# First products of a conformer/MoE block on x laid out turned and unscaled, later turned rows mostly through ScalarE, and strip groups from the highest down

## The chip, the cores and the metric

One core of a Trainium2 chip runs the whole program. The metric is the device time of one execution, in microseconds (us). A gain or a loss is told against the median of the runs of the kernel before.

## What is computed

One residual block on x of 1024 tokens by 1024 channels, float32. The lines of the reference that matter here:

```python
u = rms_norm(h, norm1_g)
proj = u @ w_in                                   # 1024 x 1792
conv_out = conformer_conv_group(proj[..., :c0], ...)   # GLU, 31 taps, LayerNorm, swish
attn_out = swa_sink_attention(q, k, v, ...)       # 8 heads, windows of two chunks
h = h + concatenate([conv_out, attn_out]) @ w_out
v = rms_norm(h, norm2_g)
h = h + moe(v, ...)                               # top 4 of 32 experts, clamped SwiGLU
```

The RMS norm divides each token's row by its root mean square and multiplies each channel by norm1_g. The division is one number per token, the gain one per channel. A product `u @ w_in` is therefore the product of `x * norm1_g` with the weights, each token's row of the result then scaled by its own number.

## The kernel before, in words

P is 128. Tokens are cut into 8 tiles of 128 (t), channels into 8 tiles of 128 (k), and tokens also into two halves of 512 (h). The program is written by hand: each of the five engines has its own list of instructions, run in order, and semaphores tie them together. SyncE (SP) issues the loads, in program order, on one queue.

**Start.** SP loads x tiles 0 to 3 into `xin`, then 128 gate and 128 value columns of w_in (`load_cv(0, 0, P)`), nine small rows, x tiles 4 to 7, b1, router weights, sinks and router bias (`small`), then the other columns of w_in. ScalarE squares each x tile with a sum (L599), GpSimd turns the sum into a reciprocal root (L450, L451), VectorE scales the tile (`norm_x`, L927). TensorE turns it in 128x128 blocks (`trans_first` L1306, `trans_u` L1332) into PSUM banks. ScalarE and VectorE take half of the banks each into `uT`, with the gain (`take_uT`, L604 and L932). `gated` (L1342) multiplies 128 columns of w_in with a half of uT: the gate side and the value side of a unit. A unit is one channel tile c of the convolution and one half h, numbered i = 2c + h, so there are eight. Units 0 and 1 are made at the start (EARLY = 2), six more in the attention loop. `turn_cols` (L1313, L1315) and `turn_b1` (L1322) turn small vectors into columns.

**Convolution.** A unit's gate goes through a sigmoid on ScalarE (`take_gate`, L620), the value is copied (`take_val`, L623), and GpSimd multiplies the two into `zT` (`glu`, L489). ScalarE writes tap 0 (`tap_zero`, L628). The other 30 taps are multiply-adds on VectorE (`tap`, L982), one after another, over 512 tokens or over both halves at once (1024). `some_taps(n, ...)` issues taps until 2n halves are done; the calls are placed by hand between other duties of VectorE.

**Attention.** A loop over s, the eight token tiles. TensorE's order in a step: `proj_kv(s+1)` (L1388), gate product of a unit, `trans_q(s)` (L1398, L1401), `proj_q(s+1)` (L1378), value product, `scores(s)` (L1416), with the turns of probabilities and the product with v of the step before. `trans_q(s)` waits for `qn_ready`, which VectorE gives in `norm_qk(s)`: a sum (L995), 2.5 (that is 3 double) taps while GpSimd takes the root (L450, L451), and two multiplications (L1002, L1005). Step 0 has VectorE issue `some_taps(16)`, `norm_qk(0)`, three more groups of taps and `norm_qk(1)`.

**Experts.** After the routing a table of passes is made on VectorE (L1169 to L1196), its end is one product on TensorE. Then a loop over passes: each takes up to 256 tokens of one expert, in widths n of 96 to 256. Hidden products (L1243) fill the time, then `down_rows` for the first 128 tokens (L1260, two halves of the columns) and `down_quads` for the others (L1278), in strips of 32 tokens; a strip group g is one such strip, in bank 3 or 7 by `quad_bank(g)`. ScalarE takes each result with its gate (L570, L577), VectorE adds the bias (L903, L910), and GpSimd adds rows to the output in DRAM by indirect DMAs: `add_rows` (L430), and, in passes that are not 128 wide, four `add_quads` (L434), one for each group, used or not. In before the groups go from 0 up: the unused ones are the last.

```python
            if n >= P:
                down_rows(0)
                down_rows(1)
...
                down_quads(range((SLOTS - n) // QG_ROWS - QUADS, QUADS) if n < P else range(-(-(n - P) // QG_ROWS)))
```

## Time and profile before

| | |
|---|---|
| median of 3 runs | 1938.51 us (1937.95 to 1939.67) |
| the profiled execution's own time | 1937.04 us |
| its span in the trace | 1935.3 us, so 1.7 us lie around it |
| granted TensorE clock, mean | 0.994 |
| TensorE (PE) busy | 98% of the span |
| VectorE (DVE) busy | 53% |
| ScalarE (ACT) busy | 23% |
| GpSimd (POOL) busy | 25% |
| moved by DMA | 519 MB, 268 GB/s over the span |

All times are us from the start of the span. A row of the chain of waits is a piece of the work that ended last, followed back. A timeline row begins with the start and the length of a run of equal instructions; in brackets stands the idle time before it and what ended it. A row of windows gives, for a stretch, the busy time of PE, of its weight loads (PEld), DVE, ACT and POOL, then the granted clock (1.00 is 2.4 GHz, 0.50 is 1.2 GHz), the DMA engines' share and GB/s.

### The profile page before, as it was taken

How to read it: one execution, taken by the hardware profiler on the slowest of the kernel's cores; microseconds unless marked ns; L12 is line 12 of the kernel's file. 1: busy time of each engine (PE TensorE's matmuls, PEld its weight loads, DVE VectorE, ACT ScalarE, POOL GpSimd, SP SyncE). 2: the span in 40 equal slices, each digit the busy share in tenths (PEclk: the TensorE clock that was granted, in tenths of full speed). 3: DMA queues.
4: the chain of work that ended last, by engine and by line, in shares of the span. 5: the costliest groups of instructions: out<-in, count | busy, mean ns of one | idle time of the engine just before them, and what ended most of it. 6: DMA issues, size and time to landing. Idle time of an engine off the chain costs nothing.

```text
span 1935.3 us, 35973 instructions
## 1 busy us (share of the span) xinstructions
PE 1900.7 (98%) x12864; PEld 1447.9 (75%) x12865; DVE 1027.2 (53%) x2836; ACT 440.0 (23%) x966; POOL 479.3 (25%) x446
## 2 busy tenths in 40 slices
PE   8999999989999999999999999999999999999997
PEld 5555554458888877888887777888888888778995
DVE  5999973365555545555554444444444444335542
ACT  4357582121111111211111111111111111111110
POOL 3110100011122211211222133333333332323333
PEclk9999999989999999999999999999999999999999
DMA  7000226348999999999999999999999998879992
GB/s 249 1 1 1 66 65 236 113 175 292 343 348 354 341 354 353 352 345 338 355 354 341 345 318 325 313 310 310 310 309 304 314 296 283 261 239 359 348 355 48
DMA packets 250502, 518.92 MB, mean 268 GB/s; under 512 B 13457, under 2 KB 30893, under 8 KB 250448
## 3 DMA queue, kind: packets, MB, share of 16 engines
q1 hardware_dynamic: 223392, 453.50, 65.0%
q0 software_dynamic: 27040, 64.66, 13.5%
q8 instruction: 39, 0.64, 0.1%
q14 instruction: 15, 0.12, 0.0%
q10 hardware_dynamic: 16, 0.00, 0.0%
HBM read 483.49 MB, written 34.62 MB: 268 GB/s over the span
## 4 chain that ended last, share of the span: by engine, by line
PE 93%; DVE 4%; ACT 1%; DMA 1%; POOL 1%; issue 1%; DVEq 0%; POOLq 0%
PE bank L1243 51%; PE bank L1260 21%; PE bank L1466 6%; PE bank L1342 4%; PE bank L1278 4%; DVE arena L982 2%; PE bank L1378 2%; PE bank L1388 1%; DMA arena<-token_rows,idx_q 1%; PE bank L1416 1%; PE bank L1636 1%; PE bank L1491 0%; PE bank L1569 0%; PE bank L1440 0%; PE bank L1306 0%
## 5 line engine op out<-in xcount | busy, mean ns | idle before, releaser
L1243 PE MATMUL bank<-arena 128*128 128x128 f32 (+6 forms) x8192 | 1001.3, 284 | 2.6 <-ACT arena L803 1.3
L1243 PEld LDWEIGHTS bank<-arena 128*128 128x128 f32 x8192 | 986.6, 191 | 16.8 <-issue 13.1
L425 POOL DMA_INDIRECT arena<-token_rows,idx_q x256 | 250.0, 977 | 638.5 <-PE bank L1243 592.6
L1260 PE MATMUL bank<-arena 128*128 128x512 f32 x928 | 403.0, 592 | 0.0
L1260 PEld LDWEIGHTS bank<-arena 128*128 128x128 f32 x928 | 174.3, 190 | 208.1 <-issue 208.1
L841 DVE TENSOR_SCALAR arena<-bank,b1c 128x256 f32<-128x256 f32 x256 | 123.8, 484 | 374.4 <-PE bank L1243 370.0
L562 ACT ACTIVATE arena<-arena 128x256 f32<-128x256 f32 x256 | 106.7, 417 | 832.5 <-DVE arena L841 832.5
L982 DVE SCALAR_TENSOR_TENSOR arena<-arena,cols 128x512 f32<-128x512 f32 (+1 forms) x226 | 182.3, 807 | 12.8 <-ACT arena L628 5.8
L890 DVE STREAM_TRANSPOSE arena<-arena 128x256 f32<-128x256 f32 x256 | 87.3, 408 | 190.5 <-DMA arena<-token_rows,idx_q 190.5
L430 POOL DMA_INDIRECT out<-arena,idx_cur x32 | 56.0, 1750 | 412.7 <-DVE arena L903 366.5
L853 DVE SCALAR_TENSOR_TENSOR arena<-arena 128x256 f32<-128x256 f32 x256 | 108.9, 425 | 38.0 <-DVE arena L850 9.8
L570 ACT ACTIVATE arena<-bank,gate_cur 128x512 f32<-128x512 f32 x64 | 43.6, 686 | 351.2 <-PE bank L1260 351.2
L843 DVE TENSOR_SCALAR arena<-bank,b1c 128x256 f32<-128x256 f32 x256 | 121.6, 475 | 0.0
L434 POOL DMA_INDIRECT out<-arena,idxq_cur x68 | 108.9, 1602 | 41.0 <-DVE arena L910 25.4
L1466 PE MATMUL bank<-arena 128*128 128x512 f32 x256 | 115.6, 599 | 0.8 <-ACT arena L699 0.8
L1342 PE MATMUL bank<-arena 128*128 128x512 f32 x256 | 113.2, 595 | 0.3 <-DVE arena L932 0.3
L850 DVE TENSOR_TENSOR arena<-arena 128x256 f32<-128x256 f32 x256 | 107.4, 419 | 2.9
L1278 PE MATMUL bank<-arena 128*32 128x256 f32 x1664 | 93.3, 380 | 0.0
L903 DVE SCALAR_TENSOR_TENSOR arena<-arena,gate_cur 128x512 f32<-128x512 f32 x64 | 47.9, 752 | 80.8 <-ACT arena L570 69.6
L1342 PEld LDWEIGHTS bank<-arena 128*128 128x128 f32 x256 | 47.5, 190 | 55.0 <-issue 54.6
L1466 PEld LDWEIGHTS bank<-arena 128*128 128x128 f32 x256 | 46.8, 190 | 52.7 <-issue 52.6
L1278 PEld LDWEIGHTS bank<-arena 128*32 128x32 f32 x1664 | 52.3, 110 | 43.7 <-issue 10.6
(240 smaller groups left out, 1089.5 us busy)
## 6 DMA issues: line engine op xcount, KB each, us to landing
arena<-in_w SPq DMA_DIRECT2D x192, 2048.0 KB, 13.5
arena<-in_b SPq DMA_DIRECT2D x32, 512.0 KB
arena<-in_x SPq DMA_DIRECT2D x16, 512.0 KB, 5.8
token_rows<-arena SPq DMA_DIRECT2D x8, 576.0 KB, 3.2
out<-arena SPq DMA_DIRECT2D x8, 512.0 KB, 6.0
arena<-in_b SPq DMA_DIRECT2D x128, 32.0 KB
arena<-token_rows,idx_q POOLq DMA_INDIRECT x256
arena<-in_w_in SPq DMA_DIRECT2D x2, 1536.0 KB, 10.7
```

The source lines that it names most:

```text
L425: pool.indirect_dma_start(out=gath_q[:, g, :], out_offset=None, in_=quads_d, in_offset=bass.IndirectOffsetOnAxis(ap=idx_q[:, g:g + 1], axis=0)
L434: pool.indirect_dma_start(out=out_q, out_offset=bass.IndirectOffsetOnAxis(ap=idxq_cur[:, g:g + 1], axis=0), in_=ytq[:, g, :], in_offset=No ...
L841: v.tensor_scalar(g1[:, r, :], bank[r][:, 0:SLOTS], b1c[:, m:m + 1], LIMIT, ALU.add, ALU.min).then_inc(g1_ready, 1)
L843: v.tensor_scalar(l1[:, r, :], bank[r][:, SLOTS:], b1c[:, MT + m:MT + m + 1], LIMIT + 1.0, ALU.add, ALU.min).then_inc(hid_free, 1)
L850: v.tensor_tensor(tt[:, r, :], g1[:, r, :], sg[:, r, :], ALU.mult).then_inc(dve_loop, 1)
L853: v.scalar_tensor_tensor(act[:, m, :], l1[:, r, :], 1.0 - LIMIT, tt[:, r, :], ALU.max, ALU.mult).then_inc(act_ready, 1)
L982: link(v.scalar_tensor_tensor(out_, zT[:, c, lo + j:lo + j + n], col(CW + c * WIDTH + j), out_, ALU.mult, ALU.add))
L1243: last = mm(bank[m % 2][:, side * SLOTS + at:side * SLOTS + at + n], w1_sb[:, k, lo:lo + P], xT[:, k, at:at + n], start=k == 0, stop=k == ...
L1260: last = mm(bank[4 + b][:], act[:, m, 0:P], w2_sb[:, m, b * HALF:(b + 1) * HALF], start=m == 0, stop=m == MT - 1)
L1278: last = mm(dst[j * QG_ROWS:(j + 1) * QG_ROWS, at:at + D // 4], act[:, m, lo:lo + QG_ROWS], w2_sb[:, m, j * (D // 4):(j + 1) * (D // 4)], ...
L1342: last = mm(dst[:], w_cv[:, k, lo:lo + P], uT[:, k, h * HALF:(h + 1) * HALF], start=k == 0, stop=k == KD - 1)
L1466: last = mm(bank[mixed_bank(t) + b][:], src, w_o[:, k, b * HALF:(b + 1) * HALF], start=part_ == 0 and i == 0, stop=part_ == 1 and i == CT - 1)
```

## The change

Four things change together.

**First products.** The host lays out x turned (`x_turned`, channels by tokens) and the first 2x128 columns of w_in, tile by tile (`w_first`). SP loads half 0 of the turned x straight into `uT`, in eight pieces, then the value side of w_first; ScalarE's queue loads the gate side. VectorE multiplies each piece by the gain in place (`apply_gain`). The products of units 0 and 1 so run on unnormed x. The token's factor comes later: `spread_x` (four transposes of a broadcast column for each half) puts the factors of all tokens on all partitions, ScalarE copies them to `rsB`, and GpSimd multiplies gate and value by them before the sigmoid and the GLU (`early_glu`, three multiplications a half instead of one). The x tiles themselves are loaded too, tiles 0 to 3 before half 1 of the turned x and tiles 4 to 7 behind it.

**Later turned rows.** `uT` is then written again from turned, normed tiles, half 0 (`trans_u(0)`) after both early units, half 1 (`trans_u(1)`) in step 0 of the attention loop, behind `trans_q(0)`. Of each four turned groups ScalarE takes three and VectorE the fourth: its `take_uT(3)` and `take_uT(7)` stand behind 12 taps, `take_uT(11)` and `take_uT(15)` behind `norm_qk(0)`. ScalarE norms x tiles 4 to 7, VectorE tiles 0 to 3. `proj_kv(0)` waits for all groups of half 0.

**Constants.** norm, bias, tap and b1 vectors come laid out as columns: `turn_cols`, `turn_b1` and their nine loads go. b1 and router weights are loads of 128 long rows. q/k/v columns of w_in are loaded before the rest of the gate and value columns.

**Experts.** Strip groups go from 3 down: groups 3 and 2 between the two row halves, 1 and 0 behind them, on all engines; unused groups are now the first. In the table, two reductions (`dead`, `wraps`) move behind `diag_ready`.

```diff
+            for k in range(KD):
+                sp.dma_start(uT[:, k, 0:HALF], x_turned[k * P:(k + 1) * P, 0:HALF]).then_inc(xt0_in[k], 16)
+            for b in range(2):
+                load_first(sp, 0, b)
             load_x(range(4))
-            load_cv(0, 0, P)
-            for dst, src in as_rows:
-                sp.dma_start(dst, src).then_inc(rows_in, 16)
+            for b in range(KD // 2):
+                sp.dma_start(uT[:, 2 * b:2 * b + 2, HALF:], x_turned[2 * b * P:2 * (b + 1) * P, HALF:]
+                             .rearrange("(k p) s -> p k s", p=P)).then_inc(xt1_in[b], 16)
             load_x(range(4, NT))
             for dst, src in small:
                 sp.dma_start(dst, src).then_inc(small_in, 16)
-            load_cv(1, P, D_CONV - P)
             sp.dma_start(w_qkv, w_in[:, 2 * D_CONV:].rearrange("(k p) n -> p k n", p=P)).then_inc(wqkv_in, 16)
+            for side in (1, 0):
+                at = side * D_CONV + P
+                sp.dma_start(w_cv[:, :, at:at + D_CONV - P], ...).then_inc(wcv_in, 16)
...
+            def apply_gain(k, h):
+                u = uT[:, k, h * HALF:(h + 1) * HALF]
+                v.tensor_scalar(u, u, col(G1 + k), None, ALU.mult).then_inc(gained, 1)
...
+            def early_glu(h):
+                half = slice(h * HALF, (h + 1) * HALF)
+                pool.wait_ge(rs_spread, h + 1)
+                pool.wait_ge(glu_ev, 2 * (h + 1))
+                pool.tensor_tensor(sigb[:, h, :], sigb[:, h, :], rsB[:, half], ALU.mult).then_inc(gate_scaled, 1)
+                link(pool.tensor_tensor(valb[:, h, :], valb[:, h, :], rsB[:, half], ALU.mult))
+                pool.wait_ge(early_sig, h + 1)
+                pool.tensor_tensor(zT[:, 0, PAD + h * HALF:PAD + (h + 1) * HALF], sigb[:, h, :], valb[:, h, :], ALU.mult
+                                   ).then_inc(z_ready, 1)
...
-            some_taps(16, EARLY)
+            some_taps(6, EARLY)
+            for g in range(3, KD, 4):
+                take_uT(g)
+            some_taps(8, EARLY)
             norm_qk(0, EARLY)
+            for g in range(KD + 3, 2 * KD, 4):
+                take_uT(g)
...
+            def all_turned(h):
+                pe.wait_ge(ut_act, 6 * (h + 1))
+                pe.wait_ge(ut_dve, 2 * (h + 1))
+            def trans_u(h):
+                pe.wait_ge(u_ready, 4 * (h + 1))
...
+                for g in range(h * KD, (h + 1) * KD):
+                    if g >= 4:
+                        if g % 4 < 3:
+                            pe.wait_ge(ut_act, 3 * (g // 4 - 1) + g % 4 + 1)
+                        else:
+                            pe.wait_ge(ut_dve, g // 4)
...
+            gated(0, 1, bank[1])
+            gated(0, 0, bank[0]).then_inc(glu_mm, 1)
+            spread_x(0)
+            gated(1, 1, bank[3])
             gated(1, 0, bank[2]).then_inc(glu_mm, 1)
-            pe.wait_ge(wcv_in[1], 32)
+            trans_u(0)
+            spread_x(1)
...
-                    for g in range(QUADS):
-                        pool.wait_ge(yq_ready, q_quads + g + 1)
+                    for g in reversed(range(QUADS)):
+                        pool.wait_ge(yq_ready, q_quads + QUADS - g)
...
+            if used < QUADS:
+                pe.sem_inc(yq_mm, QUADS - used)
...
+            if used > 2:
+                down_quads((3, 2))
+            if n >= P:
+                down_rows(1)
+            if used > 0:
+                down_quads((1, 0))
```

**TensorE, from its first real work to the attention loop's step 0.** L1306 and L1332 turn x, L1313 to L1322 turn small vectors, L1342 is `gated`, L1388 and L1378 are the first key/value and query products. Before:

```order
L1306 MATMUL bank<-ident,arena 128x128 x32
L1342 MATMUL bank<-arena 128x512 x8
L1313 MATMUL bank<-ident,arena 128x30
L1315 MATMUL bank<-ident,arena 128x31 x4
L1342 MATMUL bank<-arena 128x512 x4
L1332 MATMUL bank<-ident,arena 128x128 x16
L1342 MATMUL bank<-arena 128x512 x4
L1332 MATMUL bank<-ident,arena 128x128 x16
L1322 MATMUL bank<-ident,arena 128x128 x4
L1342 MATMUL bank<-arena 128x512 x16
L1388 MATMUL bank<-arena 128x256 x8
L1378 MATMUL bank<-arena 128x512 x8
```

Now (L1352 is `gated`, L1382 `spread_x`, L1373 `trans_u`, L1422 and L1411 the key/value and query products, L1434 and L1437 `trans_q(0)`):

```order
L1352 MATMUL bank<-arena 128x512 x16
L1382 MATMUL bank<-ident,rs 128x128 x4
L1352 MATMUL bank<-arena 128x512 x16
L1373 MATMUL bank<-ident,arena 128x128 x32
L1382 MATMUL bank<-ident,rs 128x128 x4
L1422 MATMUL bank<-arena 128x256 x8
L1411 MATMUL bank<-arena 128x512 x8
L1422 MATMUL bank<-arena 128x256 x8
L1352 MATMUL bank<-arena 128x512 x8
L1434 MATMUL bank<-ident,arena 128x128 x4
L1437 MATMUL bank<-ident,arena 128x128
L1373 MATMUL bank<-ident,arena 128x128 x32
```

The products of the early units moved ahead of all turns of x; the first 32 turns stand behind them, the other 32 behind `trans_q(0)`.

**VectorE, from the last scaling of a constant to `norm_qk(1)`.** Before (L968 is the last work on b1, L982 are taps, L995, L1002 and L1005 are `norm_qk`):

```order
L968 TENSOR_SCALAR b1T<-b1T 128x32x8
L982 SCALAR_TENSOR_TENSOR arena<-arena,cols 128x512 x16
L982 SCALAR_TENSOR_TENSOR arena<-arena,cols 128x1024 x8
L995 TENSOR_REDUCE ss<-arena 128x10
L982 SCALAR_TENSOR_TENSOR arena<-arena,cols 128x1024 x3
L1002 TENSOR_TENSOR arena<-arena,rs 128x512
L1005 TENSOR_TENSOR arena<-arena,rs 128x128
L982 SCALAR_TENSOR_TENSOR arena<-arena,cols 128x1024 x3
L982 SCALAR_TENSOR_TENSOR arena<-arena,cols 128x512 x16
L995 TENSOR_REDUCE ss<-arena 128x10
```

Now (L1003 the last work on b1, L1017 taps, L987 `take_uT`, L1030, L1037 and L1040 `norm_qk`):

```order
L1003 TENSOR_SCALAR b1T<-b1T 128x32x8
L1017 SCALAR_TENSOR_TENSOR arena<-arena,cols 128x512 x12
L987 TENSOR_SCALAR arena<-bank,cols 128x512 x2
L1017 SCALAR_TENSOR_TENSOR arena<-arena,cols 128x512 x4
L1017 SCALAR_TENSOR_TENSOR arena<-arena,cols 128x1024 x6
L1030 TENSOR_REDUCE ss<-arena 128x10
L1017 SCALAR_TENSOR_TENSOR arena<-arena,cols 128x1024 x3
L1037 TENSOR_TENSOR arena<-arena,rs 128x512
L1040 TENSOR_TENSOR arena<-arena,rs 128x128
L987 TENSOR_SCALAR arena<-bank,cols 128x512 x2
L1017 SCALAR_TENSOR_TENSOR arena<-arena,cols 128x1024 x5
L1017 SCALAR_TENSOR_TENSOR arena<-arena,cols 128x512 x13
```

The four evictions of turned groups moved in between the taps; three of the 46 taps of the first channel tile now run inside `norm_qk(1)`, where none ran before.

## Rows read from the trace of the kernel before

**Rows 1.** The page: busy shares, and the chain by engine.

```profile
PE 1900.7 (98%) x12864; PEld 1447.9 (75%) x12865; DVE 1027.2 (53%) x2836; ACT 440.0 (23%) x966; POOL 479.3 (25%) x446
...
PE 93%; DVE 4%; ACT 1%; DMA 1%; POOL 1%; issue 1%; DVEq 0%; POOLq 0%
```

**Rows 2.** The chain of waits in order of time, 0 to 105 us: start, length, what.

```profile
0.83 3.58 DMA arena<-in_x
...
14.07 7.10 PE bank L1342 x16
...
37.08 0.76 DVE arena L982
...
88.96 0.66 PE bank L1398 x4
```

**Rows 3.** Timeline of TensorE, 45 to 125 us.

```profile
46.17 3.62 PE L1388 MATMUL bank<-arena 128*128 128x256 f32 x16
49.62 7.03 PE L1378 MATMUL bank<-arena 128*128 128x512 f32 x16
...
67.34 0.66 PE L1398 MATMUL bank<-ident,arena 128*128 128x128 f32 x4 [0.37 <-DVE arena L1005]
...
88.96 0.66 PE L1398 MATMUL bank<-ident,arena 128*128 128x128 f32 x4 [1.96 <-DVE arena L1005]
```

**Rows 4.** Timelines of VectorE and GpSimd, 36 to 90 us.

```profile
61.86 3.92 DVE L982 SCALAR_TENSOR_TENSOR arena<-arena,cols 128x1024 f32<-128x1024 f32 x3
...
62.03 1.18 POOL L450 TENSOR_SCALAR ss<-ss 128x10 f32<-128x10 f32 x1 [12.85 <-DVE ss L995]
63.30 3.00 POOL L451 TENSOR_TENSOR rs<-ss,mhalf 128x10 f32<-128x10 f32 x1
...
83.76 0.82 DVE L995 TENSOR_REDUCE ss<-arena 128x10 f32<-128x640 f32 x1
...
98.06 7.00 DVE L982 SCALAR_TENSOR_TENSOR arena<-arena,cols 128x512 f32<-128x512 f32 x9
```

**Rows 5.** Timeline of all engines, 0 to 62 us.

```profile
9.61 0.75 DVE L927 TENSOR_SCALAR arena<-arena,rs 128x1024 f32<-128x1024 f32 x1 [0.73 <-POOL rs L451]
...
13.09 2.42 ACT L604 ACTIVATE arena<-bank,cols 128x512 f32<-128x512 f32 x4 [2.93 <-PE bank L1306]
...
25.07 1.91 PE L1332 MATMUL bank<-ident,arena 128*128 128x128 f32 x16
...
33.76 1.26 DVE L964 TENSOR_SCALAR rw<-rw,cols 128x32 f32<-128x32 f32 x8
...
35.65 0.69 DVE L968 TENSOR_SCALAR b1T<-b1T 128x256 f32<-128x256 f32 x1
```

**Rows 6.** Windows while the loads of the start run.

```profile
13.00:18.00 5.00, 4.68 (x16) 2.33 (x15) 3.75 (x9) 3.18 (x5) 3.73 (x12) 1.00 1.00 372
20.00:22.00 2.00, 2.00 (x9) 0.87 (x8) 0.92 (x2) 1.83 (x3) 1.53 (x4) 1.00 0.43 64
22.00:38.00 16.00, 16.00 (x65) 9.15 (x64) 8.87 (x25) 6.32 (x10) 4.21 (x5) 1.00 1.03 378
```

**Rows 7.** Windows around two falls of the granted clock.

```profile
402.00:405.00 3.00, 0.56 (x2) 0.00 (x0) 2.63 (x11) 0.05 (x1) 0.00 (x0) 1.00 0.05 22
405.40:408.40 3.00, 2.89 (x49) 2.21 (x48) 2.37 (x8) 0.97 (x3) 0.74 (x2) 0.50 0.77 298
...
425.90:432.30 6.40, 5.07 (x25) 4.98 (x24) 1.30 (x8) 2.48 (x3) 0.00 (x0) 0.50 1.05 394
```

**Rows 8.** Timeline of the tail: the last row addition and the last strip addition.

```profile
1918.31 1.62 POOL L430 DMA_INDIRECT out<-arena,idx_cur  x1 [13.09 <-DVE arena L903]
...
1928.58 1.55 POOL L434 DMA_INDIRECT out<-arena,idxq_cur  x1 [0.30 <-issue]
```

**Rows 9.** The expert loop and its head: a window, and a piece of the timeline ahead of the first pass.

```profile
400.00:1935.00 1535.00, 1513.41 (x11403) 1241.59 (x11401) 745.34 (x2341) 246.85 (x492) 421.57 (x363) 0.99 0.92 314
...
424.75 0.76 DVE L1203 COPY arena<-arena 128x512 f32<-128x512 f32 x2
```

More of the change, by code:

```diff
@@ L482, in _ @@
             pool.sem_inc(consts, 1)
-            for t in range(4, NT):
-                x_rsqrt(t)
+            pool.memset(S, NEG).then_inc(s_clear, 1)
             def glu(i):
@@ L590, in link @@
                 a.wait_ge(act_own, own[0])
-            a.dma_start(rows30[0:8, :], norm1_g.rearrange("(r c) -> r c", r=8)).then_inc(g1_in, 16)
+            a.dma_start(cols[:], columns).then_inc(cols_in, 16)
+            for b in range(2):
+                load_first(a, 1, b)
             def square_x(t):
@@ L715, in _ @@
             take_kv(0)
+            for t in range(4, NT):
+                a.wait_ge(xrs, t + 1)
+                a.activation(xin[t], xin[t], ACT.Copy, scale=rs[:, 0, t:t + 1]).then_inc(u_ready, 1)
             take_q(0)
@@ L725, in _ @@
                 take_qT(s)
+                if s == 0:
+                    for g in range(KD, 2 * KD):
+                        if g % 4 < 3:
+                            take_uT(g)
                 if s >= 1:
@@ L1162, in _ @@
             ROUNDS = P // NE
-            left, tier, circ, keys, hits = (cand[:, i, :] for i in range(5))
+            left, tier, circ, keys, hits, gone, behind = (cand[:, i, :] for i in range(7))
             EXPERT, BASE, OWN_KEY, OWN_CIRC, AT, RUN, WRAP, TIER, PACK = range(9)
@@ L1262, in down_rows @@
                 last.then_inc(yt_mm, 1)
+            first, used = (1, QUADS) if n < P else (0, -(-(n - P) // QG_ROWS))
             def down_quads(groups):
```

319 lines of the change are left out of this document (158 added, 161 removed).

## The prediction

> **What bounds the kernel now.** I read the busy shares first, then the chain of waits. TensorE is busy 98% of the span and makes 93% of the chain [rows 1]. In the expert loop it is busy 1513.4 of 1535 us [rows 9]. So a change can win only where TensorE starts late, waits, or where work lies behind its last product. There are three such places: the first 14 us, in which the products of `gated` have not begun [rows 2]; the attention loop's steps 0 and 1; and the tail behind the last strip.
>
> The second place needs the chain in order of time. From 37.1 to 89.0 us the chain is VectorE's, tap after tap, and it ends where TensorE gets `trans_q(1)` at 88.96 [rows 2]. The timeline of TensorE says how tight the two are: it waits 0.37 us at `trans_q(0)` and 1.96 at `trans_q(1)` [rows 3], 2.3 in all since 14.07. Behind 88.96 TensorE is without a gap through the steady steps. **The moment at which `trans_q(1)` runs is thus what the start is worth**, and both engines have to be followed up to it.
>
> **TensorE alone.** Between 14.07 and 88.96 it does 74.9 - 2.3 = 72.6 us of work. The small turns go (1.0), 32 turns of x that ran before 14.07 come in (twice 1.8, by 1.91 for 16 with their tail [rows 5]), and 8 spreading turns (0.9): 76.1 us. The first product could begin near 5 us, when a first piece of 0.26 MB has landed and its gain is applied; the gain's duration for 512 columns is about 0.4 by the 0.75 us for 1024 [rows 5]. It is paced by its loads, and I put the end of unit 0's products (13.7 us of work) at 18.5. The spread of tiles 0 to 3 needs their squares: loads of 5.3 MB, 17.2 us, and 2 for square, root and wait make 19.5 (the rate is below). So TensorE could have all 76.1 us done at 18.5 + 1 + 62.4 = 82, 7 us ahead of before. It won't, because in five places it now waits for an eviction that stands in a list behind other work.
>
> **VectorE's taps begin when the small loads are in.** Taps follow the scaling of router weights and b1, 1.26 and 0.69 us [rows 5], and those wait for `small`. Ahead of and in `small` the queues now carry 4.2 MB of turned x, 4.2 MB of x, 1.05 MB of w_first and 0.5 MB of constants: 9.9 MB, where before it was 5.8. The rate in stretches without holes is 372 and 378 GB/s [rows 6]. The first x tile, 0.52 MB, landed at 4.41 [rows 2], which is 3.0 us above its 1.4 us at this rate. So `small` is in at 3.0 + 26.5 = 29.5 and taps begin at **31.5**, against 37.08 before [rows 2]. VectorE's other new work fits ahead of it: the last piece of turned x lands near 23.5, then a gain and four tiles at 0.75 end at 27, and GpSimd and ScalarE have tap 0 of unit 0 at about 26.
>
> The Trainium skill puts a limit on these loads (DMA: Bandwidth & Descriptors, "Where 436 GB/s comes from"): for traffic between HBM and SBUF a core gets about 358 GB/s. By that figure, as an estimate, `small` would be in 1.2 us later and every number below with it. The trace does not bear it out: the 16 us window at 378 GB/s stands above it.
>
> **From there to `trans_q(1)`**, each step by its row:
> - 12 taps at 0.78 (7.00 for 9 [rows 4]): 9.4, to 40.9. TensorE has been parked at group 7 since about 37.5, since that bank needs group 3 taken by VectorE.
> - Eviction of group 3, four turns, eviction of group 7: 0.7 + 0.5 + 0.7 = 1.9, to 42.8. Now `proj_kv(0)` may start; before it started at 46.17 [rows 3], so 3.4 us are won so far.
> - TensorE: key/value 3.45, query 6.87, key/value 3.45, gate 6.87 (starts of neighbours in [rows 3]): 20.6, to 63.4. The gate and value columns are behind 13.1 MB and later 16.2 MB, so in by about 46; that load hides. VectorE has done the rest of its taps and `norm_qk(0)` at 63.3, just in time. The three GpSimd multiplications for unit 1 hold tap 0 of its second half to about 49; VectorE then waits some 3 us at its double taps, but those lie inside this stretch.
> - `trans_q(0)` 0.6 and 16 turns 1.8: 65.8. VectorE has stood idle since 63.3 for `take_uT(11)`.
> - `take_uT(11)`, then a wait for group 15: ScalarE takes groups at 0.6 (2.42 for four [rows 5]) and each of its banks holds up the next turn. 2.9 us until `take_uT(15)` is done, to 68.7. This was not there before.
> - Five double taps at 1.31 (3.92 for three [rows 4]) and 13 single ones: 16.7, to 85.4.
> - `norm_qk(1)`: before 88.96 - 83.76 = 5.2 [rows 2, 4], with VectorE empty while GpSimd took the root. Now three taps run beside it, as in `norm_qk(0)`, where GpSimd took 1.18 + 3.00 [rows 4]. I take 6.6 (5.2 to 7.2), to **92.0**.
>
> That is 3.1 us later than 88.96. VectorE started 5.6 us sooner, but got 2.8 us of evictions and some 6 us of waits for TensorE and ScalarE in a stretch that it bounded. TensorE waits 3 us at `trans_q(1)` instead of 1.96.
>
> **The clock.** TensorE's idle before group 7 is some 4 us, with only short turns around it. Before, an idle of 2.4 us between 402 and 405 was followed by a clock of 0.50 for 3.0 us, and a stretch of short work and waits near 423 by 6.4 us at 0.50 [rows 7]. An idle of 1.96 us at 87 was followed by none. Half of a stretch at 1.2 GHz is lost: 1.5 us by the nearest row, 0 to 3.2 as bounds. I take **1.5**, all of it on the path, since `proj_kv(0)` follows. The Trainium skill (TensorE: Matmul & The Clock Gate, "What's actually happening") calls 1.2 GHz the default state, which activity lifts; by that the fall is certain here and the sum keeps its 1.5, and without a fall it would be 1.5 less.
>
> **Head of the expert loop.** Two reductions leave the way to `diag_ready`, 0.6 us. They now stand ahead of the copies L1203, which still start at 424.75 [rows 9] and feed the turns that TensorE does last. I count 0; bounds -0.6 and +0.3.
>
> **Expert loop.** TensorE's work is the same in another order, and no engine it waits for gets more. 0 us; its idle there outside head and tail is about 2 us, all at the narrow passes, so the bounds are -1 and +2 (a new wait of ScalarE's or of a bank in some pass).
>
> **Tail.** The last pass is 192 wide, so two groups are used. GpSimd adds rows at 1918.31 and begins its last strip at 1928.58 [rows 8], having waited twice for a group to be computed. Now groups 3 and 2 are unused and ready when it gets there, and 1 and 0 are ready by 1924.1, before their turn. The row addition 1.62 + 0.30, then strips every 1.86: the last begins at 1925.8. **-2.8 us**; between 0, if what follows is held by the DMAs' landing alone, and -2.8.
>
> **Sum.** +3.1 + 1.5 + 0 + 0 - 2.8 = +1.8. On the profiled execution's 1937.04 that is 1938.8; that execution lies 1.5 below the median, 1938.51, so I predict **1940.3**. A measurement of this kernel tells about 0.2% (3.9 us) from no change, so this counts as no change.
>
> **Rivals.**
> 1. *The taps start later (slower).* Before, the queue had a hole at 20 to 22 us, 64 GB/s [rows 6], when SP was held in an issue. If the new list of small pieces (512 byte rows of w_first) is held likewise, or the rate is 330, `small` is in at 33 or 34: +4 us on every later number, 1944.5. It decides from about 33.6 on, where the whole sum passes +3.9. For it: two such holes before. Against: the new queue holds large loads while SP waits. The same result comes from 6.4 us of low clock with both waits. Chance 0.22.
> 2. *Mild side.* Loads at 400 GB/s (taps at 29.8), no fall of the clock, GpSimd's root at 5.5: 1.8 - 1.7 - 1.5 - 1.1 = -2.5, 1936.0. Chance 0.18.
> 3. *TensorE decides (faster).* If VectorE comes to its evictions as soon as TensorE turns, at 36, `trans_q(1)` is at 82 to 84, -6; with the tail -8.8, 1929.7. It needs taps from 26 on and a `norm_qk(1)` that is early. Against it: 9.9 MB cannot be in by then at any rate of the trace. Chance 0.07.
> 4. *The strips bring nothing*, because the last landing and not the last issue sets the end: 1943.1. Chance 0.05.
> The forecast itself has 0.48.
>
> **Numbers.** Rivals 1 and 4 and the upper edge of the forecast give slower by over 0.2% (above 1942.4): 0.28. Rival 3 and the edge of 2 give faster (below 1934.6): 0.11. Within: 0.61. The range leaves out rival 3 and the far end of 1: 1935.0 to 1946.0.
>
> **What would show it.** Right: `proj_kv(0)` near 43, an idle of TensorE before group 7, a clock of 0.50 around 41 to 46, idle of VectorE before `take_uT(11)`, `trans_q(1)` at 92, then the same steps shifted; GpSimd's last strip 7.5 us behind its row addition instead of 10.3. Wrong: first tap before 29 or after 34, no idle at group 7, `trans_q(1)` below 89, or a changed length of the loop's passes.

## The result, and the profile after

| | before | the change |
|---|---|---|
| median of 11 runs each | 1938.68 us (1936.43 to 1940.35) | 1943.68 us (1941.17 to 1946.01) |
| ratio, 95% interval | | 1.0021 (1.0012 to 1.0029) |
| profiled execution's own time, span | 1937.04, 1935.3 | 1946.01, 1944.2 |
| mean granted clock in it | 0.994 | 0.993 |

The change costs 5.0 us on the medians, 0.26%, and 0.21% by the ratio. The interval lies wholly above 1, so it is a loss, about as large as the 0.2% that the prediction took for the least that can be told. By its own line for slower, 1942.4, the median counts as slower, which had a chance of 0.28, and not as no change, which had 0.61. The forecast was 1940.3, in a range of 1935.0 to 1946.0: the time lies in the range, 3.4 us above the forecast. The profiled execution is the highest of its 11 runs. What in it is the change and what is chance has to be kept apart.

The page of the change, busy shares and chain by engine, against [rows 1]:

```profile
PE 1904.1 (98%) x12862; PEld 1451.1 (75%) x12863; DVE 1033.6 (53%) x2840; ACT 448.1 (23%) x978; POOL 481.0 (25%) x450
...
PE 93%; DVE 3%; DMA 1%; issue 1%; ACT 1%; SPq 1%; POOL 0%; POOLq 0%; DVEq 0%
```

Nothing of the result can be seen there. It is in the timelines. TensorE of the change, 0 to 105 us, against [rows 3]. L1373 are the turns of x, L1422 key/value products, L1411 query, L1352 gate, L1434 `trans_q`:

```profile
7.67 15.74 PE L1352 MATMUL bank<-arena 128*128 128x512 f32 x32 [7.67 <-DMA arena<-in_w_first]
...
43.82 0.66 PE L1373 MATMUL bank<-ident,arena 128*128 128x128 f32 x4 [2.67 <-DVE arena L987]
...
45.41 5.35 PE L1422 MATMUL bank<-arena 128*128 128x256 f32 x16 [0.50 <-DVE arena L987]
50.60 7.03 PE L1411 MATMUL bank<-arena 128*128 128x512 f32 x16
...
67.79 0.60 PE L1434 MATMUL bank<-ident,arena 128*128 128x128 f32 x4
...
96.02 0.66 PE L1434 MATMUL bank<-ident,arena 128*128 128x128 f32 x4 [3.60 <-DVE arena L1040]
...
96.67 8.68 PE L1352 MATMUL bank<-arena 128*128 128x512 f32 x16
105.19 3.17 PE L1411 MATMUL bank<-arena 128*128 128x512 f32 x7
```

`trans_q(1)` runs at 96.02, where it was at 88.96 [rows 3]. The gate product behind it takes 8.5 us instead of 6.9. The query product behind that starts at 105.19, against 96.43 before, **8.76 us late**. The row of before:

```profile
96.43 7.03 PE L1378 MATMUL bank<-arena 128*128 128x512 f32 x16
```

This distance then holds: 8.76 still at 400 us, 8.35 in the expert loop up to 1747.

VectorE of the change, against [rows 4]. L982 scales x tiles, L1001 the router's weights, L1017 are taps, L987 evictions of turned x, L1030 to L1040 `norm_qk`:

```profile
26.63 4.75 DVE L982 TENSOR_SCALAR arena<-arena,rs 128x1024 f32<-128x1024 f32 x4
...
32.20 1.26 DVE L1001 TENSOR_SCALAR rw<-rw,cols 128x32 f32<-128x32 f32 x8
...
33.58 9.40 DVE L1017 SCALAR_TENSOR_TENSOR arena<-arena,cols 128x512 f32<-128x512 f32 x12
43.01 0.75 DVE L987 TENSOR_SCALAR arena<-bank,cols 128x512 f32<-128x512 f32 x1
44.51 0.75 DVE L987 TENSOR_SCALAR arena<-bank,cols 128x512 f32<-128x512 f32 x1 [0.75 <-PE bank L1373]
...
65.14 0.28 DVE L1040 TENSOR_TENSOR arena<-arena,rs 128x128 f32<-128x128 f32 x1
70.28 0.75 DVE L987 TENSOR_SCALAR arena<-bank,cols 128x512 f32<-128x512 f32 x1 [4.85 <-PE bank L1373]
72.40 0.75 DVE L987 TENSOR_SCALAR arena<-bank,cols 128x512 f32<-128x512 f32 x1 [1.37 <-PE bank L1373]
73.07 16.80 DVE L1017 SCALAR_TENSOR_TENSOR arena<-arena,cols 128x1024 f32<-128x1024 f32 x18
89.90 0.82 DVE L1030 TENSOR_REDUCE ss<-arena 128x10 f32<-128x640 f32 x1
```

The engine with the most to do before `trans_q(1)` stands idle for 6.2 of the 7 us from 65.4 to 72.4, around two evictions. Nothing else was in its list until they were done.

The granted clock of the change (the column behind POOL's; its neighbours are DMA share and GB/s), against [rows 7]:

```profile
44.00:46.00 2.00, 1.50 (x10) 1.20 (x10) 1.45 (x3) 0.60 (x1) 0.38 (x1) 0.84 0.79 279
46.00:48.00 2.00, 2.00 (x6) 1.65 (x5) 1.96 (x2) 0.63 (x1) 2.00 (x2) 0.50 0.10 36
48.00:50.00 2.00, 2.00 (x9) 1.67 (x9) 1.96 (x2) 0.00 (x0) 1.92 (x2) 0.81 0.00 0
98.00:100.00 2.00, 2.00 (x3) 0.66 (x2) 1.47 (x4) 1.97 (x3) 0.00 (x0) 0.51 0.00 0
```

Two falls to 1.2 GHz, one behind each of TensorE's long waits (2.67 and 3.60 us). From `proj_kv(0)` to `trans_q(0)` it is 22.38 us, where at full clock it is 20.7 (`e5_evict_scalar`, below), and from `trans_q(1)` to the query product 9.17 instead of 7.47: 1.7 us each.

The tail, against [rows 8]: the last strip begins 7.54 us behind the row addition, where it was 10.27.

```profile
1928.97 1.62 POOL L431 DMA_INDIRECT out<-arena,idx_cur  x1 [13.09 <-DVE arena L938]
...
1936.51 1.55 POOL L435 DMA_INDIRECT out<-arena,idxq_cur  x1 [0.30 <-issue]
```

One more piece of this trace comes and goes between executions: in the passes of width 96, at 1789.73, TensorE waits 1.79 us for rows that were gathered late and turned by VectorE, where before it waited 0.65. Between 1747 and that product 1.9 us are lost, 2.3 up to the last row addition. Such a wait is absent in the traces of the next two versions; in `e11_fill_attention` it is there with 1.47 us.

### The profile page after: what moved, and what is told of

Its sections match the earlier page's. It is cut to its first block, busy times and chain, and to the rows that moved or that the text cites. A ratio compares the mean times of both kernels' runs of the same rounds, so it can differ in the third digit from the quotient of the medians.

```text
span 1944.2 us, 36152 instructions
## 1 busy us (share of the span) xinstructions
PE 1904.1 (98%) x12862; PEld 1451.1 (75%) x12863; DVE 1033.6 (53%) x2840; ACT 448.1 (23%) x978; POOL 481.0 (25%) x450
## 4 chain that ended last, share of the span: by engine, by line
PE 93%; DVE 3%; DMA 1%; issue 1%; ACT 1%; SPq 1%; POOL 0%; POOLq 0%; DVEq 0%
PE bank L1283 51%; PE bank L1300 20%; PE bank L1503 6%; PE bank L1352 4%; PE bank L1320 4%; PE bank L1411 2%; DVE arena L1017 2%; PE bank L1422 1%; DMA arena<-in_x_turned 1%; PE bank L1453 1%; PE bank L1676 0%; DMA arena<-token_rows,idx_q 0%; PE bank L1528 0%; PE bank L1609 0%; PE bank L1477 0%
## 5 line engine op out<-in xcount | busy, mean ns | idle before, releaser
L1017 DVE SCALAR_TENSOR_TENSOR arena<-arena,cols 128x512 f32<-128x512 f32 (+1 forms) x226 | 184.1, 815 | 12.9 <-ACT arena L637 6.0
L431 POOL DMA_INDIRECT out<-arena,idx_cur x32 | 52.0, 1626 | 415.4 <-DVE arena L938 233.9
L1352 PE MATMUL bank<-arena 128*128 128x512 f32 x256 | 116.2, 609 | 7.7 <-DMA arena<-in_w_first 7.7
L435 POOL DMA_INDIRECT out<-arena,idxq_cur x68 | 106.7, 1569 | 20.7 <-issue 20.7
L1352 PEld LDWEIGHTS bank<-arena 128*128 128x128 f32 x256 | 49.0, 195 | 64.9 <-issue 63.0
L1320 PEld LDWEIGHTS bank<-arena 128*32 128x32 f32 x1664 | 56.6, 110 | 40.9 <-issue 12.3
L945 DVE SCALAR_TENSOR_TENSOR arena<-arena,gq_cur 128x256 f32<-128x256 f32 x128 | 57.3, 480 | 44.3 <-ACT arena L589 44.3
```

What stands on the lines that cost most here:

```text
L435: pool.indirect_dma_start(out=out_q, out_offset=bass.IndirectOffsetOnAxis(ap=idxq_cur[:, g:g + 1], axis=0), in_=ytq[:, g, :], in_offset=No ...
L1017: link(v.scalar_tensor_tensor(out_, zT[:, c, lo + j:lo + j + n], col(CW + c * WIDTH + j), out_, ALU.mult, ALU.add))
L1320: last = mm(dst[j * QG_ROWS:(j + 1) * QG_ROWS, at:at + D // 4], act[:, m, lo:lo + QG_ROWS], w2_sb[:, m, j * (D // 4):(j + 1) * (D // 4)], ...
L1352: last = mm(dst[:], w_cv[:, k, lo:lo + P], uT[:, k, h * HALF:(h + 1) * HALF], start=k == 0, stop=k == KD - 1)
```

## The experiments

Where not said otherwise, each kernel ran 11 times beside 25 to 33 runs of before on its chip, whose medians were 1938.6 to 1938.9. "The query start" is the start of `proj_q(2)`, behind the gate product of step 1: 96.43 before, 105.19 in the change.

**Strips and start, apart.** The change has two parts that touch nothing in common (the constants and the two moved reductions go with the start). `e1_strips_only` is before with the new order of the strip groups:

```diff
-                    for g in range(QUADS):
-                        pool.wait_ge(yq_ready, q_quads + g + 1)
+                    for g in reversed(range(QUADS)):
+                        pool.wait_ge(yq_ready, q_quads + QUADS - g)
```

and the same on the other engines. `e2_start_only` is the change with the old order.

> The kernel before, with the new strip order alone. Theory of the start (the whole loss is made by 105 us, the strips win in the tail): 2.8 us faster than before, near 1935.9, the last strip addition begins 7.5 us behind the row addition instead of 10.3, and the loop's passes keep their lengths. Rival, strips cost (in the traces of before and after, 2.4 us were lost in the three narrow passes and 1.0 in the last landing): within 1 us of before, with a wait of TensorE for gathered rows behind the first narrow pass that is 1.8 us longer.

> The changed kernel with the strip groups going up again, as before. Theory of the start: 2.8 us slower than the changed kernel, near 1946.5, trans_q(1) at 96 us. Rival, strips cost: equal to the changed kernel or faster than it, near 1943.

Measured: strips alone 1936.02 (1934.53 to 1938.26), ratio 0.9985 (0.9976 to 0.9994), 2.8 below before. The start alone (7 runs) 1945.03 (1942.30 to 1946.26), ratio 1.0029 (1.0018 to 1.0040), 6.2 above. GpSimd's tail with strips alone:

```profile
1919.10 1.62 POOL L430 DMA_INDIRECT out<-arena,idx_cur  x1 [13.10 <-DVE arena L905]
...
1926.64 1.55 POOL L434 DMA_INDIRECT out<-arena,idxq_cur  x1 [0.30 <-issue]
```

Again 7.54 us, without the two waits of before. So the strips win 2.8 us and the start loses some 6. The two add up to 3.4, the change shows 5.0; the difference is within the intervals of three medians.

The start-only kernel also tells chance from change in the start: its first product begins at 7.23, its taps at 33.06, its `proj_kv(0)` runs at full clock, `trans_q(1)` is at 93.84 and the query start at 103.00. Over three executions of this start (the change, this one, and `e11_fill_attention`, whose start is the same) `trans_q(1)` is at 96.02, 93.84, 94.90. Before's start gave 88.96 and 88.73.

**Evictions earlier in VectorE's list.** `e3_evict_early`: VectorE takes groups 3 and 7 behind 7 taps instead of 12.

```diff
-            some_taps(6, EARLY)
+            some_taps(3.5, EARLY)
             for g in range(3, KD, 4):
                 take_uT(g)
-            some_taps(8, EARLY)
+            some_taps(10.5, EARLY)
```

> The changed kernel; VectorE takes turned groups 3 and 7 behind 7 taps instead of 12, the other 5 taps after them. If the place of VectorE's evictions parks TensorE: proj_kv(0) at 41 instead of 45.4, no idle of 2.7 us at group 7 and no clock of 0.50 behind it, trans_q(1) at 90 instead of 96, 6 us faster than the changed kernel, near 1937.5. If VectorE's total work up to trans_q(1) bounds and places do not matter: the five taps come back later, trans_q(1) stays within 1 us of 96, and the time is unchanged.

Measured: 1944.8 (1939.49 to 1950.73), 1.003 (1.0019 to 1.0041). TensorE:

```profile
41.80 3.69 PE L1422 MATMUL bank<-arena 128*128 128x256 f32 x16 [0.50 <-DVE arena L987]
...
65.45 1.12 PE L1434 MATMUL bank<-ident,arena 128*128 128x128 f32 x4 [2.77 <-DVE arena L1040]
...
94.83 0.66 PE L1434 MATMUL bank<-ident,arena 128*128 128x128 f32 x4 [3.60 <-DVE arena L1040]
```

`proj_kv(0)` is 3.6 us earlier and at full clock, but TensorE then waits 2.77 us at `trans_q(0)`, where the change did not wait: VectorE is done with `norm_qk(0)` at 65.39, and was at 65.42 in the change. `trans_q(1)` at 94.83 lies among the three executions of the change's start. My theory that the place of the first two evictions mattered fell. It is VectorE's whole row of work and waits that counts, wherever TensorE is let go.

**The clock, kept up.** `e4_keep_clock` puts products on the identity that nobody reads into the two waits: 22 before group 7, 30 before `trans_q(1)`.

```diff
+                            if g == 7:
+                                for _ in range(22):
+                                    mm(bank[5][:, 0:P], ident[:], ident[:], start=True, stop=True)
                             pe.wait_ge(ut_dve, g // 4)
```

> The changed kernel; TensorE fills its two long waits (at group 7, before trans_q(1)) with products of the identity, nothing else moves. If the two falls of the granted clock behind these waits cost what the trace shows (5.35 instead of 3.45 us, 8.47 instead of 6.87): 3.5 us faster, near 1940.2, and proj_kv(0) takes 3.5 us. If the waits alone make the loss: unchanged, 1943.7, or up to 1 slower by filling products that run past the release.

Measured (7 runs): 1944.41 (1942.51 to 1945.77). The clock stayed at 1.00 at both places, but each product is two instructions of 0.115 us: the fillers took 5.1 and 6.9 us and overran the waits, `trans_q(1)` came at 98.22. The test was too blunt. `e7_keep_clock_sized` has 15 and 14.

> The change, with products on the identity that nobody reads (128 columns, 0.115 us each by the earlier such run) in the two waits of TensorE: 15 ahead of the last group's wait of turned x (1.7 us in a wait of 2.7), 14 ahead of trans_q(1)'s (1.6 us in a wait of 3.6). They end before the wait does, so they delay nothing. Theory (the two falls of the granted clock to 0.50 follow from the two waits, and cost 1.9 us in proj_kv(0) and 1.6 in the gate product): both stretches at 1.00, trans_q(1) at 95.1 to 96.0, gate product 6.9 in place of 8.5, median 1.6 to 3.5 us below the change: 1940.2 to 1942.1. Rival (the first fall lies beside VectorE's work and costs nothing at trans_q(1), and the fillers are too few to keep the clock): 1943.7.

Measured: 1943.2 (1940.35 to 1946.4), 1.0023 (1.0014 to 1.0032). Both places at 1.00, `trans_q(1)` at 94.76, the gate product 6.9, the query start at 102.23: 3.0 earlier than in the change's own trace, 1.8 earlier than the mean of the three executions of this start (105.19, 103.00, 103.79). The median moved by 0.5 only. The fillers were counted at half their length: 15 products took 3.4 us and not 1.7, and ended 1.5 us behind the eviction of group 3 (done at 42.7), so that VectorE got group 7 late:

```profile
40.93 3.51 PE L1373 MATMUL bank<-ident 128*128 128x128 f32 x30
```

```profile
44.92 0.75 DVE L987 TENSOR_SCALAR arena<-bank,cols 128x512 f32<-128x512 f32 x1 [2.17 <-PE bank L1376]
```

VectorE's wait was 0.75 in the change. So "they delay nothing" was wrong for the first wait. That the falls cost time there is shown by the rows; that they cost it in the median is not.

**All evictions on ScalarE.** `e5_evict_scalar`:

```diff
-                        if g % 4 < 3:
-                            take_uT(g)
+                        take_uT(g)
```

on ScalarE for both halves, VectorE's four calls removed.

> The change as it is, but ScalarE evicts all 16 groups of turned x (4 turned tiles each) and VectorE none. Theory (in this kernel VectorE's own work up to norm_qk(1) bounds trans_q(1): taps in a row behind its two gains, plus two evictions of half 0, two of half 1 and the waits of the latter on TensorE): VectorE loses 43.01 to 45.18 and 70.28 to 73.07 (2.2 + 2.8 us) and both idle stretches ahead of them (0.75 and part of 4.85), proj_kv(0) begins at 41 to 42 with the clock at 1.00, and trans_q(1) stands at 89 to 91 in place of 96.02, with no wait of over 1 us and no low clock ahead of the gate product. Row addition and end 6 to 8 us earlier than the change: median 1936 to 1938. Rival (VectorE only waits for what TensorE gives, and ScalarE's own queue is then the slow one): ScalarE's four further evictions at 0.6 us hold the turns, trans_q(1) moves by under 2 us, median 1942 to 1944.

Measured: **1934.8** (1933.59 to 1937.35), ratio 0.9978 (0.9969 to 0.9987): 3.9 below before, 8.9 below the change. TensorE:

```profile
42.59 3.69 PE L1411 MATMUL bank<-arena 128*128 128x256 f32 x16 [1.31 <-ACT arena L623]
...
69.77 7.11 PE L1400 MATMUL bank<-arena 128*128 128x512 f32 x16 [1.74 <-ACT arena L623]
...
88.73 0.60 PE L1423 MATMUL bank<-ident,arena 128*128 128x128 f32 x4
```

No wait at `trans_q(1)`, no low clock in the start. VectorE is done with `norm_qk(1)` at 84.49, 11.5 us sooner than in the change: some 7.0 us were its waits for TensorE, 2.8 the four evictions, 1.0 a multiplication (L1037) that no longer ran beside GpSimd's, and 0.8 an earlier first tap. ScalarE's cost is the two short waits. The query start, 96.14, is that of before's start (96.20 in `e1_strips_only`): freed of VectorE's waits, the new start is as fast as the old one and not faster.

**Only the second half's evictions on ScalarE.** `e9_scalar_half1` asks which waits they were.

> The change, but ScalarE evicts all eight groups of the second half of turned x, where VectorE's two evictions wait on TensorE; the first half stays 6 and 2. Theory (VectorE's row up to norm_qk(1) is the bound, and its two waits behind trans_u(1), 4.85 and 1.37 us of idle with 1.5 us of evictions, are the larger part of what the change lost): VectorE goes from norm_qk(0) at 65.5 straight into its 18 taps and is done with norm_qk(1) at about 88.5, and trans_q(1) then stands on TensorE's own work: 91 to 92.5 in place of 96.02, with no idle of over 0.5 us ahead of it, and the gate product behind it at 1.00 (6.9 in place of 8.5). The first fall of the clock, in proj_kv(0), may stay. Median 4 to 5.5 us below the change: 1938.2 to 1939.7, level with before. Rival (it is the first half's wait that costs, and the second half's stands beside other work): trans_q(1) moves by under 1.5 us, median 1942 to 1944.

Measured: 1937.83 (1935.15 to 1939.64), ratio 0.9999 (0.9990 to 1.0008): level with before, 5.85 below the change. VectorE, then TensorE:

```profile
66.08 16.80 DVE L1016 SCALAR_TENSOR_TENSOR arena<-arena,cols 128x1024 f32<-128x1024 f32 x18
```

```profile
92.05 0.60 PE L1433 MATMUL bank<-ident,arena 128*128 128x128 f32 x4
```

The 18 tap instructions start 7 us sooner, and TensorE no longer waits at `trans_q(1)`: 4.0 us are won there and 1.7 by the clock behind it. Two of VectorE's evictions, 11 and 15, were most of the change's loss. The first two are worth the other 3 us.

**Small scalings later.** `e6_late_consts` moves the scaling of router weights and b1 to step 2.

> The change, but VectorE scales the router's weights (eight instructions, 32.20) and adds one to b1 (33.37) at step 2, behind the whole start, so that its taps follow the normalisation of x. Theory (VectorE's row of work up to norm_qk(1) has no slack, and it is not the small loads that the taps wait for): the taps begin at about 32.2 in place of 33.58, trans_q(1) at 94.6 in place of 96.02, median 1.4 us below the change: 1942.3. Rival (a load or TensorE sets the start of each stretch): taps or trans_q(1) where they are, median 1943.7.

Measured: 1941.18 (1939.13 to 1944.52), 1.0014 (1.0005 to 1.0023), 2.5 below the change. Taps begin at 31.36, `trans_q(1)` at 92.14, the query start at 101.30. That is more than the 1.4 us of scalings: the wait before group 7 shrank to 0.84 us as well, and the clock stayed up behind it. `e8_scalar_late` has this and the edit of `e5_evict_scalar`.

> Both edits at once: ScalarE evicts all groups of turned x, and the router's weights and b1 are scaled at step 2. Theory (VectorE's row of work bounds trans_q(1)): the two gains add up until TensorE's own work binds, trans_q(1) at 88 to 90, median 1935 to 1937, at or below that of before with only the new order of the strips (1936.02). Rival: no better than the better one of the two edits alone, since TensorE or ScalarE binds by then.

Measured: 1935.1 (1933.35 to 1936.32), `trans_q(1)` at 88.86. The rival was right: once TensorE is the bound, 1.4 us less on VectorE are worth nothing.

**Products by piece.** `e10_by_piece` is `e8_scalar_late`, and starts each product of `proj_kv(0)` as soon as its own group is evicted, and those of `proj_q(1)` from the fifth group on. The banks of the second half's groups are dealt in another order for it. The edit at `proj_kv`:

```diff
-                all_turned(s // 4)
                 for k in range(KD):
+                    pe.wait_ge(ut_act, s // 4 * KD + k + 1)
```

> The version of the last batch with all evictions on ScalarE and the late scaling of the router's weights, and with it proj_kv(0) and proj_q(1) start each of their eight products as soon as the group of turned x that it reads is evicted, not behind the last one (for the second half the banks of the groups are dealt as 4, 0, 1, 3, so that bank 4 is free for proj_q(1) early). Theory (with VectorE off the path, the start is bound by TensorE, and its two idle stretches of 1.31 and 1.75 us ahead of these products are all that is left on it): both idle stretches under 0.5 us, trans_q(1) at about 86 in place of 88.86, median about 3 us below that version: 1932. Rival (VectorE's norm_qk(1) at 84.4 or ScalarE's evictions bind again at once): trans_q(1) at 88 to 89, median 1934 to 1935.

Measured: 1935.09 (1932.04 to 1937.89). Both waits are gone and the query start is at 94.70, 1.6 sooner than in `e8_scalar_late`. But the time is the same, and the mean clock of its runs is 0.993 where that of `e8_scalar_late` is 0.996. In the traces the gain goes between 240 and 270 us, where the clock falls:

```profile
253.00:255.00 2.00, 2.00 (x11) 1.31 (x11) 1.93 (x3) 1.67 (x5) 1.55 (x1) 0.81 0.00 0
255.00:257.00 2.00, 2.00 (x11) 2.00 (x12) 1.97 (x4) 0.00 (x0) 0.00 (x0) 0.50 0.00 0
```

**Where the scatter comes from.** The stretch from `mean_sum(0)` to the spread of the LayerNorm scale is the same work in every kernel. In the change it starts at 252.68 and ends at 274.90:

```profile
252.68 3.60 PE L1516 MATMUL bank<-arena,ones_ln 128*128 128x512 f32 x8
...
274.90 0.60 PE L1536 MATMUL bank<-ident,lnr 128*128 128x128 f32 x4
```

22.2 us, as before in its trace. In `e4_keep_clock` the same pair stands at 253.13 and 273.47, 20.3 us:

```profile
253.13 3.60 PE L1523 MATMUL bank<-arena,ones_ln 128*128 128x512 f32 x8
...
273.47 0.65 PE L1543 MATMUL bank<-ident,lnr 128*128 128x128 f32 x4 [0.46 <-POOL lnr L521]
```

At a clock of 1.00 it took 20.3 (also in `e5_evict_scalar` and `e8_scalar_late`), with a fall 22.2 to 25.6: 22.2 in `e9_scalar_half1`, 24.7 in `e1_strips_only` and `e2_start_only`, 25.6 in `e3_evict_early`, `e6_late_consts` and `e7_keep_clock_sized`, 25.4 in `e10_by_piece`. Up to 5 us, as much as the whole result. Two other places scatter as well. The first hidden product of the expert loop (x96, at 428 before) took 10.8 us in six of the fourteen traces and 12.3 to 13.0 in the others, and from the first pass of width 96 to the last row addition the same work took 179.4 us (before) to 181.8 (the change). `e11_fill_attention` is the change with fillers in the two short waits (0.69 and 1.25 us) ahead of the fall.

> A test of where the scatter between executions comes from. In the profiles so far the stretch from the first mean sum of the conv branch (252.68 in the change) to the spread of its scale (274.90) takes 20.3 us at a clock of 1.00 and 22.2 to 25.6 where the clock falls to 0.50 behind TensorE's two waits of 0.69 and 1.25 us there, with nothing else different. This is the change, with two and five products on the identity that nobody reads (0.23 us each) in these two waits, at weigh_v(5) and in scores(6). Theory (the fall follows from the waits, it comes in some executions and not in others, and is what scatters the times): the stretch takes 20.3 to 21 us, the runs lie closer together than the change's 1941.17 to 1946.01, at 1941 to 1942.5, median 2 us below the change: 1941.7. Rival (the fall follows from the narrow products behind the waits, or from neither): the stretch at 22 to 25.6 and the runs as scattered as those of the change, median 1943 to 1944.

Measured (10 runs): 1942.79 (1940.54 to 1945.23). The fall came later, at some 265, but it came; the stretch took 21.3, and the runs are as scattered as before. The two filled waits alone are not the cause. The fall now stands at a third wait, which the fillers left:

```profile
265.18 1.11 PE L1434 MATMUL bank<-ident,arena 128*128 128x128 f32 x4 [0.66 <-DVE arena L1040]
```

The same wait stands at the fall in `e1_strips_only` and `e2_start_only`; in `e4_keep_clock`, `e5_evict_scalar` and `e8_scalar_late` it is there too and the clock stayed up. `e12_wide_sums` is `e10_by_piece` and changes the narrow products behind the waits (the reader then takes one column of each 128):

```diff
-                    last = mm(bank[4][:, t:t + 1], sqT[:, c, t * P:(t + 1) * P], ones_ln[:, 0:1], start=c == 0,
+                    last = mm(bank[4][:, t * P:(t + 1) * P], sqT[:, c, t * P:(t + 1) * P], ones_ln[:], start=c == 0,
```

> The version with products by piece, and the variance sums of the conv branch (64 products at L1518 there, one column of output each, 0.12 us) with all 128 columns of the matrix of ones in place of its first: same values, the reader takes one column of each 128. In that version the granted clock fell at 253.9, as these products began, to 0.50 until 268, and the stretch from mean sum to the spread of the scale took 25.4 us in place of the 20.3 that it takes at 1.00. Theory (TensorE's narrow products, which keep it occupied and do little, are what brings the fall there; the fillers in the two waits ahead of them did not stop it): the clock stays at 1.00 in 240 to 290, the stretch takes 20.3 to 21.5 us, and the median comes down by 3 us to 1932, mean clock 0.996 or 0.997 in all runs. Rival (the fall has to do with the waits and with what TensorE did before, or with nothing in this stretch): the stretch takes 22 to 25.5 us again in most runs, median 1935.

Measured (5 runs, 9 of before): **1932.13** (1930.66 to 1933.58), ratio 0.9965 (0.9951 to 0.9978). The same windows, and the end of the stretch, which began at 242.09:

```profile
253.00:255.00 2.00, 2.00 (x15) 1.52 (x14) 1.93 (x3) 1.57 (x5) 1.45 (x1) 1.00 0.00 0
255.00:257.00 2.00, 1.44 (x10) 1.03 (x10) 1.97 (x4) 0.21 (x1) 0.00 (x0) 1.00 0.00 0
```

```profile
262.42 0.65 PE L1526 MATMUL bank<-ident,lnr 128*128 128x128 f32 x4 [0.45 <-POOL lnr L521]
```

20.3 us, and all five runs at a mean clock of 0.995 to 0.997, where the 11 of `e10_by_piece` had 0.991 to 0.996. This is the fastest version of all, 6.5 us below before. Wide products are enough to keep the clock up from this start. That narrow ones bring it down is not shown: all runs of `e5_evict_scalar` and `e8_scalar_late` have them, at mean clocks of 0.995 to 0.997.

**All of them in one table.** Median minus query start says what lies behind the start (for `e2_start_only` 2.8 is taken off for its tail, for before too). The query start is that of one execution, the median that of all runs:

| version | query start | median | rest | median of mean clocks |
|---|---|---|---|---|
| before | 96.43 | 1938.68 | 1839.5 | 0.993 |
| e1_strips_only | 96.20 | 1936.02 | 1839.8 | 0.994 |
| e2_start_only | 103.00 | 1945.03 | 1839.2 | 0.993 |
| the change (mean of three such starts) | 103.99 | 1943.68 | 1839.7 | 0.993 |
| e3_evict_early | 103.99 | 1944.80 | 1840.8 | 0.991 |
| e4_keep_clock | 105.63 | 1944.41 | 1838.8 | 0.996 |
| e5_evict_scalar | 96.14 | 1934.80 | 1838.7 | 0.996 |
| e6_late_consts | 101.30 | 1941.18 | 1839.9 | 0.993 |
| e7_keep_clock_sized | 102.23 | 1943.20 | 1841.0 | 0.992 |
| e8_scalar_late | 96.28 | 1935.10 | 1838.8 | 0.996 |
| e9_scalar_half1 | 99.47 | 1937.83 | 1838.4 | 0.995 |
| e10_by_piece | 94.70 | 1935.09 | 1840.4 | 0.993 |
| e11_fill_attention | 103.79 | 1942.79 | 1839.0 | 0.993 |
| e12_wide_sums | 94.61 | 1932.13 | 1837.5 | 0.996 |

The start varies by 11 us, the rest by 3.5, and the rest mostly goes with the mean clock. The change itself is what it does up to the query start, 7.6 us on the mean of three, and the tail, -2.8: 4.8 of the measured 5.0.

## Why the prediction was right, and where it was off

**The mechanism held.** The start worse, the strips better, the loop unchanged, VectorE and not TensorE the bound, and the shape of each wait: TensorE idle before group 7, VectorE idle before `take_uT(11)`. The tail was forecast at -2.8: 10.27 - 7.54 = 2.73, and 2.8 on the medians of `e1_strips_only`. Rival 4 is out. So is rival 3: the taps did not begin before 31. Head of the loop 0: it starts 8.70 us late where the step at 400 us was 8.76 late, so the moved reductions brought next to nothing; its first product then took 12.61 us against 13.01, at a mean granted clock of 0.86 instead of 0.83. Rival 1 came in part. Its queue did not stall: the small loads were in at 31.5 and not at 33 or 34, and the taps began at 33.0 to 33.6, up to its line of 33.6. But its second way, the low clock behind both waits, is what happened, with 3.4 us lost where it had 3.2, and the time, 1943.7, lies nearer to its 1944.5 than to the forecast.

**The start, by its steps.** The forecast had `trans_q(1)` at 92.0. In the change's trace it is 4.0 later:

| step | forecast | measured | off by |
|---|---|---|---|
| taps begin | 31.5 | 33.58 | +2.1 |
| 12 taps, groups 3 and 7, to `proj_kv(0)` | 11.3 | 11.83 | +0.5 |
| TensorE to `trans_q(0)` | 20.6 | 22.38 | +1.8 |
| to `take_uT(11)` | 2.4 | 2.49 | +0.1 |
| `take_uT(11)` to `(15)` | 2.9 | 2.79 | -0.1 |
| 18 tap instructions | 16.7 | 16.83 | +0.1 |
| `norm_qk(1)` | 6.6 | 6.12 | -0.5 |

The +1.8 is the first low clock, which the sum had as a term of its own, 1.5. **The step that failed is the first**: "taps begin at 31.5". I let them wait for `small`, at 29.5, and costed what VectorE has ahead of them at four tiles of 0.75. Both were short. `small` came 2 us later, at 31.5, though the loads ran at 389 GB/s from 8 us on; up to 6 us they had run at 192. And VectorE was not ready for it either: it reached L1001 at 32.20 without idle (in `e11_fill_attention` it got there at 31.4 and waited 0.20 us for `small`, so the two are nearly level). Its four tiles took 4.75 us: the first two, at 26.63 and 28.30, took 1.75 each, beside GpSimd's products for unit 0, the last two 0.74 (0.75 before [rows 5]). This row is the product beside the second tile:

```profile
27.91 1.59 POOL L502 TENSOR_TENSOR arena<-arena 128x512 f32<-128x512 f32 x1
```

The Trainium skill (SBUF — State Buffer, "SBUF: two separate sides") says that VectorE and GpSimd share a pair of ports under an exclusive lock: if VectorE's instruction is in a 2-port mode or reads two inputs from SBUF, the one of the two that starts first holds the pair for its whole instruction, and the other waits. The trace agrees: both slow tiles began behind a product of GpSimd's, and each ended 0.55 us behind its end. Whether these scalings are of the kind that it names, no run shows. `e6_late_consts` shows that this row of VectorE's has no slack: with 1.4 us of scalings out of it the taps begin at once behind the tiles, at 31.36, and the time falls by 2.5. Over the three executions of this start the first tap lies at 33.58, 33.06 and 33.01, so 1.7 of the 2.1 is the change and 0.4 chance: the first load landed later.

**The clock** was forecast at 1.5, behind group 7. There it cost 1.7 in the change's trace, 1.1 in that of `e11_fill_attention` and nothing in `e2_start_only`: 0.9 on average. So the fall was not certain, as one reading in the prediction has it: in one of three executions it did not come. What the sum left out is a second fall, behind the wait at `trans_q(1)`, in all three: 1.7, 1.7 and 1.4 us. I had a wait of 3 us there and gave its fall no term in the sum, though rival 1 names it. With +1.7 for the taps, +1.6 for the second fall and -0.6 for the first, the forecast's +1.8 becomes +4.5; measured 5.0. So the forecast was too low by two mis-sized terms of the same start, the begin of the taps and the clock; the tail and the rest stood.

**A number that did no harm**: unit 0's products were to end at 18.5 and ended at 23.25, since the first began at 7.67 and they wait for VectorE's gains. In the change VectorE is later anyway. In the versions where TensorE is the bound it counts: my 82 for TensorE alone plus these 4.8 is 86.8, and `e12_wide_sums` has `trans_q(1)` at 87.20.

**What stays open.** The 0.5 us of `e7_keep_clock_sized` against the 1.8 of its start (its trace is of its slowest execution, 1946.4); why `small` came 2 us late; and why `e8_scalar_late` keeps its clock in attention's end where `e10_by_piece`, whose query start is 1.6 us earlier, loses it in its trace and, by the mean clocks, in most runs. The Trainium skill (TensorE: Matmul & The Clock Gate, "What's actually happening") says that the chip's watch on the engine's activity runs on its own and does not start with the kernel, so that the same kernel meets it at another point each time. That would fit runs of one kernel with and without the fall; it does not by itself say why one version falls seldom, and no run here varied the start alone.

## What to carry to other kernels

An eviction given to the engine with the longest list is not 0.75 us: it is 0.75 plus the wait for its producer, with the whole list behind it. Give it to the engine that has slack, even if all of them then go one by one. Before costing an earlier start, lay out the row of the engine that has to be ready, at durations beside its neighbour's, and look at every wait of TensorE's near 2 us and above for what the clock does behind it. And when two versions differ by a few us, compare the start of one fixed instruction in the trace, and look for a stretch whose length varies between executions.

## What was not expected of the hardware

- The granted clock fell to 0.50 in windows in which TensorE's busy time was full (2.00 of 2.00 us at 255 us in `e10_by_piece`), while products with one column of output ran between wider ones. With 128 columns in each of them the stretch took 20.3 us at 1.00 instead of 25.4, as it did in `e5_evict_scalar` with one column. One column costs nearly as long as 128: 8 instructions took 0.95 us in the one case and 1.05 in the other.
- A tile's scaling on VectorE went from 0.75 to 1.75 us beside GpSimd's products, and `norm_qk`'s L1037 took 0.69 in some places and 1.69 where GpSimd's multiplication ran beside it (L486, 93.95 to 95.21 in the change); it too ended 0.55 us behind it.
- A wait alone does not tell whether the clock falls. Before group 7 a wait of 2.67 us brought 1.2 GHz for 3 to 4 us, one of 1.87 did in `e9_scalar_half1` and `e11_fill_attention`, one of 1.96 did not in `e2_start_only`. The 3.60 us ahead of `trans_q(1)` brought it in all five executions that had them without fillers.
